# One encoder layer in fp32r halves: accumulators split 512 + 256 over two banks in place of 384 + 384

## What is computed

```python
mod = silu(c) @ w_ada + b_ada                 # shift, scale, gate per group
h = modulate(rmsnorm(x, norm1_g), sh1, sc1)
proj = h @ w_in                               # 1024 -> 4352: q k v | hyena | two gates
attn = windowed_gqa_sink(q, k, v, sink)
uc = conv_b + sum(pad(proj_hy)[:, i:i + L] * conv_w[i] for i in range(3))
hy = hyena(uc, spectra)                       # long convolutions by spectra
merged = sigmoid(gate_a) * (attn @ w_attn_o) + sigmoid(gate_h) * (hy @ w_hyena_o)
x = x + g1 * (merged @ w_out)
h = modulate(rmsnorm(x, norm2_g), sh2, sc2)
x = x + g2 * (square(relu(h @ w_up)) @ w_down)   # 1024 -> 4096 -> 1024
y = modulate(rmsnorm(x, final_g), shf, scf)
```

## Time and profile before

| | us |
|---|---|
| median of 3 timed runs | 1123.1 |
| lowest and highest | 1121.71, 1123.13 |
| span of the profiled execution | 1122.6 |
| TensorE busy in it | 1092.4 |
| VectorE busy | 801.6 |
| ScalarE busy | 452.9 |
| GpSimd busy | 107.3 |

### The profile page before, as it was taken

One profiled execution on the slowest core, in us unless ns is written; L12 is line 12 of the kernel. 1 busy time (PEld: TensorE's weight loads), 2 busy tenths in 40 slices (PEclk: granted clock), 3 DMA queues, 4 the chain that ended last, 5 costly groups with the idle time before them and its releaser, 6 DMA issues. The chain is left out here.

```text
span 1122.6 us, 16641 instructions
## 1 busy us (share of the span) xinstructions
PE 1092.4 (97%) x6304; PEld 1020.8 (91%) x6304; DVE 801.6 (71%) x1335; ACT 452.9 (40%) x792; POOL 107.3 (10%) x132
## 2 busy tenths in 40 slices
PE   6989999999999999999999999999999999999996
PEld 4777788888899999999899999999999999999886
DVE  5867689989478685556455777787878778688534
ACT  5631146666632222423346232244342626157414
POOL 2101210000325332000000000000000000000000
PEclk9999999999999999999999999999999999999999
DMA  9932354443342333753312331143333322222303
GB/s 350 389 95 101 150 188 120 136 139 95 110 149 104 104 117 123 266 157 113 112 57 92 119 128 56 56 150 95 113 92 115 95 97 101 86 75 76 94 19 114
DMA packets 45525, 138.85 MB, mean 124 GB/s; under 512 B 5051, under 2 KB 10635, under 8 KB 44556
## 3 DMA queue, kind: packets, MB, share of 16 engines
q1 hardware_dynamic: 29024, 80.21, 21.6%
q0 software_dynamic: 11376, 44.84, 11.5%
q10 hardware_dynamic: 5052, 12.81, 3.3%
HBM read 121.61 MB, written 15.74 MB: 122 GB/s over the span
## 5 line engine op out<-in xcount | busy, mean ns | idle before, releaser
L740 PE MATMUL acc_ps<-act_hilo,w_hi 128*128 128x384 f32 x1536 | 338.2, 341 | 2.4 <-DVE w_lo L1712 1.6
L740 PEld LDWEIGHTS acc_ps<-act_hilo,w_hi 128*128 128x128 f32 x1536 | 269.3, 188 | 22.0 <-issue 20.0
L740 PE MATMUL acc_ps<-act_hilo,w_lo 128*128 128x384 f32 x768 | 195.3, 335 | 0.0
L740 PEld LDWEIGHTS acc_ps<-act_hilo,w_lo 128*128 128x128 f32 x768 | 138.8, 188 | 0.0
L1185 PE MATMUL acc_ps<-hidden_hilo,act_hilo 128*128 128x384 f32 x768 | 135.0, 335 | 0.6 <-DVE hidden_hilo L2274 0.4
L1185 PEld LDWEIGHTS acc_ps<-hidden_hilo,act_hilo 128*128 128x128 f32 x768 | 133.0, 188 | 1.9 <-issue 1.0
L1712 DVE TENSOR_TENSOR w_lo<-w_raw,w_hi 128x1024 fp32r<-128x1024 f32 x62 | 77.0, 1242 | 60.5 <-ACT w_hi L1261 59.6
L1261 ACT ACTIVATE w_hi<-w_raw 128x1024 fp32r<-128x1024 f32 x62 | 65.2, 1052 | 44.5 <-PE acc_ps L740 41.0
L2160 DVE SCALAR_TENSOR_TENSOR xT<-acc_ps,modT,xT 128x512 f32<-128x512 f32 (+1 forms) x32 | 19.7, 617 | 61.4 <-PE acc_ps L819 61.3
L1803 DVE CUSTOM_DVE_ANT_0 dot_out<-dot_ring,c_rows,vecT 128x1024 f32<-128x1024 f32 x48 | 61.6, 1283 | 2.6
L2285 DVE SCALAR_TENSOR_TENSOR xT<-acc_ps,modT,xT 128x384 f32<-128x384 f32 (+2 forms) x96 | 40.5, 478 | 31.4 <-PE acc_ps L1185 31.4
(11 more groups left out here) (292 smaller groups left out, 2006.4 us busy)
## 6 DMA issues: line engine op xcount, KB each, us to landing
w_raw<-in_w_pre SPq DMA_DIRECT2D x50, 512.0 KB, 3.5
dot_ring<-in_w_ada_cols POOLq DMA_DIRECT2D x48, 512.0 KB, 3.8
w_raw<-in_w_up SPq DMA_DIRECT2D x32, 512.0 KB, 4.0
w_raw<-in_w_down SPq DMA_DIRECT2D x16, 512.0 KB, 3.5
w_raw<-in_w_down_half SPq DMA_DIRECT2D x32, 256.0 KB, 2.7
spec<-filt_out POOLq DMA_DIRECT2D x12, 512.0 KB, 3.0
gate_spill<-gates_out ACTq DMA_DIRECT2D x16, 384.0 KB, 2.5
hy_spec<-spec SPq DMA_DIRECT2D x12, 512.0 KB, 5.3
```

The costliest lines, as they stand in the source:

```text
L740: mm = pe.matmul(acc_ps[:, slot, 512 * h:512 * h + HALF], w[:, kw, :], src[:, x, k, HALF * h:HALF * h + HALF], start=(first and i == 0), s ...
```

## The change

The slot's 768 tokens now lie as one stretch: columns 0 to 511 fill the first bank, 512 to 767 the first half of the second. Each pair is one matmul of 512 columns and one of 256 with the same weights, in that order, in place of two of 384. The border between the banks is now the border between the groups, so `PIECES` has two entries, 512 and 256 columns: the convolution's sides take 4 VectorE instructions per tile in place of 6, the residuals 2 in place of 3. `halves` goes, and ScalarE's instructions read and write one stretch of 768 columns. `long_k` and `short_k` are the three matmuls for 512 or for 256 columns alone, `side_k` and `group_k` call them. `gated` replaces the bodies of the residuals. The number of matmuls is the same.

```diff
-PIECES = ((0, 0, HALF), (0, HALF, TS), (1, TS, T))
+PIECES = ((0, 0, TS), (1, TS, T))
...
         def acc(s):
-            return acc_ps[:, s].rearrange("p (h n) -> p h n", n=512)[:, :, 0:HALF]
+            return acc_ps[:, s, 0:T]
         def acc_piece(s, a, b):
-            a, b = (a + 512 - HALF, b + 512 - HALF) if a >= HALF else (a, b)
             return acc_ps[:, s, a:b]
...
-            def gemm_k(slot, s, k, kw, src, first, last):
-                for i, (w, x) in enumerate(((whi[s], 0), (whi[s], 1), (wlo[s], 0))):
-                    for h in range(2):
-                        mm = pe.matmul(acc_ps[:, slot, 512 * h:512 * h + HALF], w[:, kw, :], src[:, x, k, HALF * h:HALF * h + HALF],
-                                       start=(first and i == 0), stop=(last and i == 2))
+            def long_k(slot, hi, lo, k, src, first, last):
+                to = acc_ps[:, slot, 0:TS]
+                for i, (w, x) in enumerate(((hi, 0), (hi, 1), (lo, 0))):
+                    mm = pe.matmul(to, w[:, k, :], src[:, x, k, 0:TS], start=(first and i == 0), stop=(last and i == 2))
+                return mm
+            def short_k(slot, hi, lo, k, src, first, last):
+                to = acc_ps[:, slot, TS:T]
+                for i, (w, x) in enumerate(((hi, 0), (hi, 1), (lo, 0))):
+                    mm = pe.matmul(to, w[:, k, :], src[:, x, k, TS:T], start=(first and i == 0), stop=(last and i == 2))
+                return mm
+            def gemm_k(slot, hi, lo, k, src, first, last):
+                a, b = acc_ps[:, slot, 0:TS], acc_ps[:, slot, TS:T]
+                for i, (w, x) in enumerate(((hi, 0), (hi, 1), (lo, 0))):
+                    for to, c0, c1 in ((a, 0, TS), (b, TS, T)):
+                        mm = pe.matmul(to, w[:, k, :], src[:, x, k, c0:c1], start=(first and i == 0), stop=(last and i == 2))
                 return mm
...
             def side_k(s, h, k, src):
-                for i, (w, x) in enumerate(((whi[s], 0), (whi[s], 1), (wlo[s], 0))):
-                    mm = pe.matmul(acc_ps[:, s, 512 * h:512 * h + HALF], w[:, k, :], src[:, x, k, HALF * h:HALF * h + HALF],
-                                   start=(k == 0 and i == 0), stop=(k == KD - 1 and i == 2))
-                return mm
+                return (long_k, short_k)[h](s, whi[s], wlo[s], k, src, k == 0, k == KD - 1)
...
-                    act_e.activation(halves(qk[:, t, :]), src, ACT.Copy).then_inc(acc_free[s], 1)
+                    act_e.activation(qk[:, t, :], src, ACT.Copy).then_inc(acc_free[s], 1)
...
                 for i, (_, a, b) in enumerate(PIECES):
                     a = a + 1 if a in (0, TS) else a
-                    dve.wait_ge(cv_part, 3 * m + 1 + i)
+                    dve.wait_ge(cv_part, len(PIECES) * m + 1 + i)
...
+            def gated(s, m, gate, g):
+                a, b = GROUPS[g][0], GROUPS[g][0] + GROUPS[g][1]
+                return dve.scalar_tensor_tensor(xT[:, m, a:b], acc_ps[:, s, a:b], modT[:, gate + m, g:g + 1], xT[:, m, a:b],
+                                                ALU.mult, ALU.add)
...
-                for g, a, b in PIECES:
-                    last = dve.scalar_tensor_tensor(xT[:, m, a:b], acc_piece(s, a, b), modT[:, G2 + m, g:g + 1],
-                                                    xT[:, m, a:b], ALU.mult, ALU.add)
-                last.then_inc(sd_free, 1)
+                gated(s, m, G2, 0)
+                gated(s, m, G2, 1).then_inc(sd_free, 1)
```

More of the change, by code:

```diff
@@ L889, in first @@
                 pe.wait_ge(n_lo, k + 1)
[L890 removed]
+                mm = gemm_k(s, whi[s], wlo[s], k, act, k == 0, k == KD - 1)
                 if k == KD - 1:
@@ L1182, in st_down_k @@
                 for k in ks:
[L1183 to L1187 removed]
+                    mm = gemm_k(m % 2, hi, lo, k, hid, k == 0, k == PK - 2)
                 return mm
```

41 lines of the change are left out of this document (12 added, 29 removed).

## The result

The changed kernel is slower: 1127.18 us against 1123.12 us before (medians of 10 runs each), a ratio of 1.0033 with a 95% interval of 1.0022 to 1.0043. That is 4.1 us more. It lies 4.3 us above the forecast and 2.8 above the upper end of its range, on the side to which the prediction gave 0.08.

What follows compares the result with a forecast made beforehand. TensorE, busy 1092.4 of 1122.6 us, was taken as the bound. 1122.6 + 0.0 (matmuls) - 0.47 (VectorE) + 0.32 (two tiles) = 1122.5 us; the median lies 0.5 above that span, so 1122.9, range 1121.2 to 1124.4.

Steps and rivals of the forecast that it cites:

- the side to which the prediction gave 0.08: Whole kernel: slower than before by more than 0.2% (2.2 us), chance 0.08.
- The matmuls: TensorE's 1728 pairs: 512 plus 256 columns take 346.7 ns, as 384 twice do, so 0 us.
- The price of a single change: TensorE where one length follows another: some 6 ns gained down a step, some 5 lost up.
- The dear step alone: Rival, TensorE's pairs: each long matmul pays 5 ns, the short gains nothing; +8.6 us, 1131.5 us, chance 0.06.
- ends of -10.4 and +8.6 us: Bounds of the matmul term: 1728 pairs with only the 6 ns gain, or only the 5 ns loss.
- a chance of 0.83 on the middle: The forecast's own case, matmul sum at 0: 1121.2 to 1124.4 us, chance 0.83.
- The equal 13.3 ns: TensorE's runs of 256, 384 and 512 columns: each step is its columns at 2.4 GHz plus 13.3 ns.
- VectorE's saving: 64 fewer VectorE instructions at 0.117 us save 7.5 us there, of which 0.47 us reaches TensorE.
- There is one place: Only TensorE's 1.84 us wait at 163.6 lets VectorE's saving through: -0.47 us, bounds 0 to -0.5.
- The residuals: All 40 residuals, one VectorE instruction fewer each: costed at nothing, since TensorE's work on the other slot covers them.
- The two tiles behind the norm: Behind the second norm: idle time inside shrinks, wait before next tile grows from 0.3 to some 1.1 us; +0.32 us.
- The clock: TensorE's clock: granted in full (2.4 GHz) in every slice of the profile before.

Runs made afterwards that it cites:

- the grouped kernel: Changed kernel with each tile's matmuls of 512 columns ahead of its 256: 1123.57 us against 1123.49, ratio 1.0001; with slot 1 seven blocks behind, 1122.88 us, ratio 1.0000.
- the run with TensorE's change alone: Kernel before with only lines 740 and 1185 changed to 512 and 256 columns, VectorE and ScalarE as before: 1126.89 us, ratio 1.0032.
- The last grouped version: Changed kernel grouped by tile, slot 1 seven blocks behind, every other first-down tile split at its sixth block: 1122.94 us against 1123.52, ratio 0.9993.
- mirrored: Changed kernel with the middle pair of each block turned round (512, 256, 256, 512, 512, 256 columns): 1126.89 us, ratio 1.0031.
- triples: Changed kernel with each block's three matmuls of 512 columns first, then its three of 256: 1125.54 us, ratio 1.0020.

## Why the prediction was wrong, point by point

- **The matmuls, the step that failed.** "Down a step gains some 6 ns, up a step loses some 5, and an alternation takes both in turn, so I take the sum at 0." Both halves were taken from single records at a change of length. What a steady alternation does can't be had from these: it has a fast rhythm, where the sum is indeed 0 (1.04 us per block, so 8.32 us for a tile of 48), and a slow one with 20 ns more per block (8.48 us). The term was 0, with an upper end of +8.6 us; measured was +4.6 us in the profiled execution, or 2.7 ns for each of the 1728 pairs, and 3.3 and 5.5 us in the other two (3.9 and 6.1 less the 0.6 of before).
- **The price of a single change was read too short.** The prediction took the first record behind a change. The price is spread over several matmuls: between 512 and 256 columns it is 28 ns up and 8 back down, as the grouped kernel shows. The trace of before had changes of length with a loss in it that the prediction didn't look at. TensorE's timeline of before, where 384 columns follow 512:

```profile
311.08 0.39 PE L1007 MATMUL wk<-hy_foldT_hi,dft_fwd_lo 128*128 128x512 f32 x1
311.31 0.87 PE L740 MATMUL acc_ps<-act_hilo,w_hi 128*128 128x384 f32 x4
...
312.38 0.85 PE L740 MATMUL acc_ps<-act_hilo,w_hi 128*128 128x384 f32 x4
```

  The first six matmuls take 1.07 us where six steps of 173.3 make 1.04. To the nanosecond, 26 ns are lost over 12 matmuls here and at three more places like it, on the way down, where the prediction expected a gain; and 41 ns on the way up from 384 to 512, four times (at 526.74 for one). These rows spoke for the side of a loss.
- **The rival that came nearest.** "The dear step alone" named the place and the sign and got 0.06. Its reason, weights loaded under a short matmul, isn't settled. The prediction held a load time that isn't from its rows against the short step of 120 ns. The trace has a record of each load, and that is longer than the step: 188 ns in the mean, before and after. Weight loads by line, before:

```profile
L740 PEld LDWEIGHTS acc_ps<-act_hilo,w_hi 128*128 128x128 f32 x1536 | 269.3, 188 | 22.0 <-issue 20.0 <-ACT act_hilo L1301 0.8
```

  All pairs that were tried have one matmul with a step below 188 ns, 512 and 384 columns too (173.3). Against the reason speaks that runs of 256 columns alone and pairs of 384 have steps below it as well and lose nothing. A pair with both steps above 188 ns, 512 and 464 columns for instance, was not run.
- **What I weighed too lightly** was my own remark that "in the trace 512 and 256 columns never alternate". An operation whose steady state the trace doesn't show, times 1728, with ends of -10.4 and +8.6 us, is no case for a chance of 0.83 on the middle and a range of 3.2 us.
- **The equal 13.3 ns** of three lengths was read as proof that a step depends on its own length alone. It holds inside long runs of equal length only, as lines 736 and 743 after still show.
- **VectorE's saving.** Right in size for one pass: the pass of three instructions of 1.18 us takes 1.06 us with two, as forecast, and the wait of 1.84 us is 1.27. VectorE's timeline of after, at the first convolution tile:

```profile
142.53 1.14 DVE L1959 SCALAR_TENSOR_TENSOR hy_xv<-acc_ps,vecT,hy_xv 128x511 f32<-128x511 f32 x2 [1.12 <-ACT hy_xv L1485]
143.59 1.13 DVE L1964 SCALAR_TENSOR_TENSOR hy_xv<-acc_ps,vecT,hy_xv 128x511 f32<-128x511 f32 x2
```

  TensorE's timeline of after, at the two waits that it shortened:

```profile
163.71 1.09 PE L969 MATMUL wk<-ident,att_s 128*128 128x128 f32 x8 [1.27 <-ACT att_s L1398]
...
291.47 1.08 PE L980 MATMUL wk<-att_pT,v_rows 128*64 128x256 f32 x8 [0.35 <-ACT att_pT L1406]
```

  "There is one place" was wrong. There is a second, at 294 us, where TensorE waited 1.21 us for ScalarE's line 1406. ScalarE had itself waited 2.58 us for the reciprocal, behind a convolution tile and four modulation products that VectorE works through almost without a gap from 275.86 us on. TensorE's timeline of before there:

```profile
294.00 1.08 PE L976 MATMUL wk<-att_pT,v_rows 128*64 128x256 f32 x8 [1.21 <-ACT att_pT L1406]
```

  And ScalarE's, of before:

```profile
285.11 1.71 ACT L1398 ACTIVATE att_s<-att_s,att_rden 128x256 f32<-128x256 f32 x4 [2.58 <-DVE att_rden L2000]
```

  After, TensorE waits 0.35 us there. I had followed the wait one step, to ScalarE, and stopped. With the third place at 440 us TensorE waits 0.57 + 0.86 + 0.17 = 1.6 us less, in place of 0.47. Not all of this is VectorE's doing. In the run with TensorE's change alone VectorE has its old instructions, and yet the waits are 1.77 and 0.98 us: slower matmuls come later and find less to wait for. That can account for 0.07 and 0.23 us. The one convolution tile ahead of the second wait can give 2 x 0.117 = 0.23 us; what gave the remaining 0.4 us isn't shown. The residuals brought nothing, as forecast.
- **The two tiles behind the norm.** Right: the idle time inside (0.42 us at 601.30) is gone, the next tile waits for its weights (0.95 us in its record, 1.1 counted from the last side matmul's step), and the stage costs 0.34 us where 0.32 was forecast.
- **The clock** played no part: 0.996 of full speed was granted in both.

By my estimate, with the matmul term at its fast rhythm and the waits as measured, the kernel would have come out at 1078.7 - 1.6 + 0.3 = 1077.4 us of rest, 1.3 us below before. The last grouped version gets half of that (1078.1); 20 ns for each pair of changes are part of what it still pays.

## What to carry to other kernels

In a kernel like this one, split a product over two banks into equal parts, or put the equal lengths in long runs; matmuls of unequal length that alternate cost 0.3 to 0.7% of this kernel, and not in every execution of a stage, so that one profile may show a stage without it. Price a change of length by start to start over the next ten matmuls, not by the first record. Where the trace lacks the steady state of what a change makes, and the count is in the thousands, the ends of the bound are the forecast's range. Follow a wait back past the engine that released it until you find one that was never idle.

## What the runs showed of the hardware that I had not expected

- TensorE's step in a run of equal matmuls was the columns at 2.4 GHz plus 13.3 ns for 256, 384 and 512 columns. The page "TensorE: Matmul & The Clock Gate" of the Trainium skill, section "Back-to-back issue gap", has 2.5 ns on top of the columns for an isolated matmul; no run here shows so small a step, with a weight load before each.
- Alternating lengths have several steady rhythms, apart by 20 ns per six matmuls: 0 or 20 (512 and 256; 448 and 320), almost always 20 (416 and 352; 392 and 376), 20 or 40 (512 and 384), 6.7 or 13.4 (mirrored), 10 (triples). Equal lengths had none in three traced executions.
- A single change of length also has its price, over up to nine matmuls: 28 ns from 256 to 512 columns, -8 ns back, 41 ns from 384 to 512, 26 ns from 512 to 384, 7 ns from 256 to 384.
- The rhythm was entered where a stretch began and held for up to 118 us. Eleven tiles of the projection had it or not by the matmuls ahead of them, the same in four traces. In the merge, the loops and the down products the same code had it one time and not the next. Why the steps lock so, and what in the weight loads, the reads or the writes makes the 20 ns, stays open; the records of loads and matmuls show only that both keep step with each other.
